# First attention: forget-gate bias as a row of the padded keys, output projection by rows, and the last value unit placed between the heads

## The chip, the cores and the metric

The kernel runs on one core of a Trainium2 chip. The core has a matrix engine (TensorE, PE in the profile), a vector engine (VectorE, DVE), an activation engine (ScalarE, ACT), GpSimd (POOL) and SyncE (SP), which issues most transfers. The engines run their own queues in order and wait for each other by semaphores. The metric is the device time of one execution in microseconds (us); lower is better.

## The reference

Two transformer blocks over 256 positions of width 1024, in float32. The change lies in the first layer of the first block:

```python
u = rms_norm(h, norm_mix[i]); m = rms_norm(mem, norm_mem[i])
q, k, v, f_logit, mq = split(u @ fox_w_in)          # 12 heads of 64, and 4 memory heads
q = rms_norm(q, fox_g_q); k = rms_norm(k, fox_g_k)
log_f = log_sigmoid(f_logit + fox_b_f)
c = cumsum(log_f, axis=1)
s = einsum('bqhd,bkhd->bhqk', q, k) * scale + (c[t] - c[s])   # causal
p = softmax(where(k_pos <= q_pos, s, NEG_INF)); o = p @ v
mem_out = memory_attention(mq, mk, mv, g_mq, g_mk)  # 256 memory tokens
h = h + concatenate([o, mem_out], -1) @ fox_w_out
z = rms_norm(h, norm_ffn[i]); h = h + swiglu(z, ...)
```

Behind it come a convolution layer with a mixture of experts, and a second block with differential and stick-breaking attention.

## The kernel before

**Exact products.** Each float32 weight unit (128 x 2048 numbers, 1 MB) is loaded into one of six buffers `raw`. ScalarE copies it to the reduced format (`wh`, the "hi" part, L736), then VectorE forms the rest (`wl`, "lo", L1671). This pair of instructions is called a split; there are three split buffers. `split_after(name)` splits the unit three places behind `name`, once `name` has been multiplied. A product is three matmuls (L1156 to L1158): hi x hi, hi x lo, lo x hi. Activations are split in the same way into `xh` and `xl`. A unit is 48 matmuls of 256 columns. `by_channels` and `by_tokens` multiply a unit whose columns are 256 outputs, over all 1024 inputs; `down` multiplies a unit of 256 input rows into all 1024 outputs, in four PSUM banks at once.

**Order around the change.** Units run in the order mk0, mv0, mq0 (memory), fq0 to fq2, fk0 to fk2, fv0 to fv2 (query, key, value of the 12 forget-gate heads, four heads to a unit), then 16 heads of attention (12 forget-gate, 4 memory), then fo0 to fo3 (output projection), norm sum number 2, and the feed-forward network (g0, u0, g1 and so on). During the projections, VectorE takes a reciprocal per query or key unit and scales it out of PSUM (`qk_scale`); keys go to `kz`, where each head has its 64 rows and 64 rows of zeros, so that one matmul over 128 rows can use a pair of heads' queries `qT` and see one head.

**The attention** is a loop over iterations i, written out on each engine (`attention` in the TensorE, ScalarE, VectorE code). `T_LAG` is 3 and `PV_LAG` is 4. In iteration i TensorE computes the scores of head i (L1287), for forget-gate heads with a second product that adds the bias -c[s] (L1290: `selh`, a one-hot of the head, times `negc`, the row of -c); transposes the probabilities of head i-3 (L1170); and multiplies those of head i-4 by the values (L1308, L1313). VectorE takes the scores out of PSUM into `att_p` with c[t] and the mask, but first waits for the transposes of head i-3, whose buffer it overwrites; then it takes the maxima (L1828) and the reciprocal of the row sums of head i-1. ScalarE takes the exponentials (L859) and copies the transposed head i-3 out of PSUM (L868). GpSimd scales the probabilities (L630, L632). When a pair of heads is complete, ScalarE copies it to `xh` (L873) and VectorE writes the low part `xl`.

`Sessions` assigns the PSUM banks by hand: each user of a bank waits (`claim`) until the one before has been drained. Scores alternate between banks 0 and 1, the transposes between 2 and 3, the pairs' outputs between 4 and 5. The splits that fall into the attention are placed by iteration, on both engines:

```python
FOX_SPLITS = {16: ("fv0",), 20: ("fv1", "fv2")}
attention(fox_maps, lambda i: [split_after(name) for name in FOX_SPLITS.get(i, ())])
```

So fo0 is split in iteration 16, fo1 and fo2 in 20; fo3, g0 and u0 are split while TensorE multiplies fo0 to fo3.

Of the kernel before, what the change touches and what calls it, by code (L numbers as in the profile page):

```python
# [202 lines left out]
def build(nc, x_dram, mem_dram, c_dram, cst_dram, cols_dram, main_dram, moe_dram, out):  # L203
    ctx = ExitStack()
    with ctx:
# [102 lines left out]
        selh = sqz[:, 0:FOX_HEADS * P].rearrange("p (h m) -> p h m", h=FOX_HEADS)  # L308
        negc = sqz[:, FOX_HEADS * P:FOX_HEADS * P + T]
# [41 lines left out]
        for j in range(1, 6):  # L351
            product(f"{'fq' if j < 3 else 'fk'}{j % 3}", j % 4)
            S.add(f"qsum{1 + j}", 4 + (1 + j) % 2)
        product("fv0", 7)
        S.add("qsum7", 5)
        product("fv1", 6)
        product("fv2", 2)
# [4 lines left out]
        def add_maps(kinds):  # L362
# [5 lines left out]
            dict(kind="fox" if h < FOX_HEADS else "mem", head=h, q=qT[:, h // 2, :], k=kz[:, h, :],  # L368
# [15 lines left out]
        FOX_SPLITS = {16: ("fv0",), 20: ("fv1", "fv2")}  # L384
# [4 lines left out]
        def add_attention(rng):  # L389
            n, a0 = len(rng), rng[0]  # L390
            for i in range(n + PV_LAG):
                if i < n:
                    S.add(f"sc{a0 + i}", (a0 + i) % 2)
                if 0 <= i - T_LAG < n:
                    S.add(f"pT{a0 + i - T_LAG}", 2 + (a0 + i) % 2)
                if 0 <= i - PV_LAG < n and (i - PV_LAG) % 2 == 0:
                    g = (a0 + i - PV_LAG) // 2
                    S.add(f"pv{g}", 4 + g % 2, own_signal=True)

        add_attention(fox_maps)  # L400
        for j in range(4):
            product(f"fo{j}", j)
        S.add("nsum2", 6)
# [204 lines left out]
        def _(pool):  # L608
# [11 lines left out]
            zero_keys(kz, "keys_zeroed")  # L620
            subtract_hi("x")
# [99 lines left out]
        def _(act):  # L721
# [110 lines left out]
            for j in range(6):  # L832
# [4 lines left out]
                if j == 0:  # L837

                    act.wait_ge(sem("negc_zeroed"), 1)
# [3 lines left out]
            for j in range(3):  # L843
                values_out(f"fv{j}", vv[:, :, T * j:T * j + T])
                if j == 0:
                    qk_sd(7)
            warm(ACT.Exp)

            def attention(rng, meanwhile=None, before=None):
                n, a0 = len(rng), rng[0]  # L850
                for i in range(n + PV_LAG + 1):
# [18 lines left out]
                    if 0 <= i - PV_LAG - 1 < n and (i - PV_LAG - 1) % 2 == 1 and maps[a0]["kind"] != "diff":  # L870
                        g = (a0 + i - PV_LAG - 1) // 2
# [6 lines left out]
            attention(fox_maps, lambda i: [split_after(name) for name in FOX_SPLITS.get(i, ())])  # L878

            warm(ACT.Sqrt)  # L880
            for j in range(4):
                wait_drained(act, f"fo{j}")
                square(hT, sqz, j)
                if j < 3:
                    split_after(f"fo{j}")
# [263 lines left out]
        def _(pe):  # L1149
# [125 lines left out]
            by_tokens("fv2")  # L1275

            def attention(rng, meanwhile=None):
                n, a0 = len(rng), rng[0]
                for i in range(n + PV_LAG):
                    if i < n:  # L1280
                        a = a0 + i
                        m, s = maps[a], bank(f"sc{a}")
                        full = m["kind"] == "mem"
                        claim(pe, f"sc{a}")
# [1057 lines left out]
```

## Time and profile before

| | us |
|---|---|
| median of 3 runs | 1910.46 (1907.53, 1910.46, 1910.5) |
| the profiled execution | 1907.86 |
| its span (first to last instruction) | 1906.0 |
| TensorE busy | 1802.0 (95%) |
| VectorE, ScalarE, GpSimd busy | 1443.3, 1171.6, 205.9 |
| first score of the first attention | 112.44 |
| output projection starts | 164.06 |
| root of norm sum 2 (ScalarE) | 190.83 |

In the profile's rows, L12 is line 12 of the kernel, `out<-in` are the tensors, `xN` the number of instructions merged into the row, and square brackets hold the idle time of the engine ahead of the row and the engine whose work ended it. A duration reaches to the end of the work; the next instruction of the engine can start somewhat before it. A float32 matmul counts as two instructions.

### The profile page before, as it was taken

The page shows a single profiled execution, that of the slowest core. Times are in us where ns is not written, and L with a number is a line of the kernel's source. Part 1 is how long each engine was busy: PE and PEld are TensorE (multiplying, and loading weights), DVE is VectorE, ACT ScalarE, POOL GpSimd, SP SyncE. Part 2 cuts the span into 40 slices and gives each one's busy share as a digit, 9 for nine tenths or more (in the row PEclk, how much of TensorE's full clock was granted, in tenths as well). Part 3 has the DMA queues.
Part 4 walks back from the last instruction along what each step waited for, and adds up shares of the span by engine and source line. Part 5 has one row for each costly group of instructions (what it writes and reads, how often), then busy time and mean ns, then how long its engine had stood idle before and what let it go on. Part 6 is the DMA issues. An engine that isn't in the chain of part 4 may idle for free.

```text
span 1906.0 us, 27557 instructions
## 1 busy us (share of the span) xinstructions
PE 1802.0 (95%) x10598; PEld 1583.3 (83%) x10598; DVE 1443.3 (76%) x1321; ACT 1171.6 (61%) x1141; POOL 205.9 (11%) x161
## 2 busy tenths in 40 slices
PE   6988899999899999999999999999999989689997
PEld 6977899999778878888788787887877889589997
DVE  6765687778758888888888888888889854765554
ACT  5435343455667777877777777777777744743332
POOL 2032111121120000000000000000006000403221
PEclk8999989999999999999999999999999999999999
DMA  7303798852139999999999999999999934035540
GB/s 310 136 23 145 295 400 323 317 199 89 67 142 388 373 357 390 367 385 378 360 390 364 384 376 361 391 366 382 377 358 417 370 130 155 1 121 189 177 155 23
DMA packets 74571, 520.84 MB, mean 273 GB/s; under 512 B 8064, under 2 KB 8192, under 8 KB 13952
## 3 DMA queue, kind: packets, MB, share of 16 engines
q1 hardware_dynamic: 73056, 514.02, 70.8%
q0 software_dynamic: 1440, 5.77, 0.8%
q8 instruction: 54, 0.88, 0.2%
q14 instruction: 21, 0.17, 0.0%
HBM read 504.02 MB, written 15.73 MB: 273 GB/s over the span
## 4 chain that ended last, share of the span: by engine, by line
PE 83%; DVE 7%; ACT 5%; DMA 2%; issue 2%; POOL 1%; ACTq 0%; DVEq 0%; SPq 0%
PE ps L1156 25%; PE ps L1158 24%; PE ps L1157 24%; DVE wl L1671 2%; PE ps L1358 1%; PE ps L1179 1%; DMA raw<-in_units 1%; ACT wh L1030 1%; PE ps L1526 1%; DMA raw<-in_experts 1%; DVE big L1664 1%; PE ps L1287 1%; DVE sqz L1664 1%; PE ps L1308 1%; ACT L1041 0%
## 5 line engine op out<-in xcount | busy, mean ns | idle before, releaser
L1671 DVE TENSOR_TENSOR wl<-raw,wh 128x2048 fp32r<-128x2048 f32 x446 | 1025.3, 2302 | 303.8 <-ACT wh L736 178.4
L1030 ACT ACTIVATE wh<-raw 128x2048 fp32r<-128x2048 f32 x336 | 643.2, 1918 | 180.5 <-PE ps L1158 176.5
L1156 PE MATMUL ps<-wh,xh 128*128 128x512 f32 (+1 forms) x1040 | 398.0, 383 | 9.6 <-DVE wl L1671 9.6
L1158 PE MATMUL ps<-wh,xl 128*128 128x512 f32 (+1 forms) x1040 | 390.2, 375 | 0.0
L1157 PE MATMUL ps<-wl,xh 128*128 128x512 f32 (+1 forms) x1040 | 389.7, 375 | 0.0
L1156 PE MATMUL ps<-xh,wh 128*128 128x256 f32 x1184 | 343.7, 290 | 25.0 <-DVE xl L1671 11.4
L1157 PE MATMUL ps<-xl,wh 128*128 128x256 f32 x1184 | 338.9, 286 | 0.0
L1158 PE MATMUL ps<-xh,wl 128*128 128x256 f32 x1184 | 338.7, 286 | 0.0
L736 ACT ACTIVATE wh<-raw 128x2048 fp32r<-128x2048 f32 x107 | 204.2, 1910 | 185.5 <-PE ps L1158 163.7
L1156 PEld LDWEIGHTS ps<-xh,wh 128*128 128x128 f32 x1184 | 231.4, 195 | 30.2 <-issue 23.7
L1156 PEld LDWEIGHTS ps<-wh,xh 128*128 128x128 f32 x1040 | 195.8, 188 | 50.9 <-DVE wl L1671 17.0
L1157 PEld LDWEIGHTS ps<-xl,wh 128*128 128x128 f32 x1184 | 231.6, 196 | 1.8 <-issue 1.7
L1158 PEld LDWEIGHTS ps<-xh,wl 128*128 128x128 f32 x1184 | 231.3, 195 | 0.0
L1158 PEld LDWEIGHTS ps<-wh,xl 128*128 128x128 f32 x1040 | 195.8, 188 | 35.9
L1157 PEld LDWEIGHTS ps<-wl,xh 128*128 128x128 f32 x1040 | 196.0, 188 | 34.0 <-issue 1.0
L1156 PE MATMUL ps<-wh,ah 128*128 128x512 f32 x448 | 175.9, 393 | 0.0
L1158 PE MATMUL ps<-wh,al 128*128 128x512 f32 x448 | 174.7, 390 | 0.0
L1157 PE MATMUL ps<-wl,ah 128*128 128x512 f32 x448 | 174.4, 389 | 0.0
L1156 PE MATMUL ps<-ah,wh 128*128 128x256 f32 x432 | 123.8, 287 | 6.5 <-DVE wl L1671 6.2
L1157 PE MATMUL ps<-al,wh 128*128 128x256 f32 x432 | 123.5, 286 | 0.0
L1158 PE MATMUL ps<-ah,wl 128*128 128x256 f32 x432 | 123.4, 286 | 0.0
L646 POOL TENSOR_TENSOR al<-att_p,ah 128x512 fp32r<-128x512 f32 x27 | 74.9, 2773 | 359.3 <-ACT ah L897 359.3
(292 smaller groups left out, 1933.9 us busy)
## 6 DMA issues: line engine op xcount, KB each, us to landing
raw<-in_experts SPq DMA_DIRECT2D x336, 1024.0 KB, 6.9
raw<-in_units SPq DMA_DIRECT2D x134, 1024.0 KB, 5.7
x_rows<-big SPq DMA_DIRECT2D x1, 6144.0 KB, 22.6
big<-x_rows SPq DMA_DIRECT2D x8, 512.0 KB, 7.9
y_rows<-big SPq DMA_DIRECT2D x7, 512.0 KB, 8.2
y_rows<-big SPq DMA_DIRECT2D x1, 2560.0 KB, 27.4
big<-in_mem SPq DMA_DIRECT2D x1, 1024.0 KB, 7.1
hT<-in_x SPq DMA_DIRECT2D x1, 1024.0 KB, 9.1
```

Of the source, the lines that this page charges most:

```text
L646: pool.tensor_tensor(al[:, c % 2, :], sg[:, c % 2, :], ah[:, c % 2, :].bitcast(F32), ALU.subtract).then_inc(sem("hid_lo"), 1)
L736: act.activation(wh[:, p % SPL, :], raw[:, n % RAW, :], ACT.Copy).then_inc(sem("hi_ready"), 1)
L1030: act.activation(wh[:, p % SPL, :], raw[:, n % RAW, :], ACT.Copy).then_inc(sem("hi_ready"), 1)
L1156: mm(out_, lh, rh, start=start, stop=False, **kw)
L1157: mm(out_, lh, rl, start=False, stop=False, **kw)
L1158: return mm(out_, ll, rh, start=False, stop=stop, **kw)
L1179: ins = mm(bank(f"nsum{k}")[:, 0:T], ones, src[:, T * j:T * j + T], start=(j == 0), stop=(j == KT - 1))
L1287: ins = mm(s[:, at:at + nk], m["q"][:, P * t:P * t + P], m["k"][:, 0:nk], start=True, stop=not fox)
L1308: mm(o[:, 0:T], m["v"][0], pT[:, 0:T], start=not second, stop=False, skip_group_check=True)
L1358: mm(bank(f"conv{c}")[:, 0:T], diag[:, n % DIAG_RING, :], upad[:, c, tap:tap + T], start=(tap == 0), stop=(n + 1 == taps_through(PE_CONV, ...
L1664: return V.scalar_tensor_tensor(out=out_, in0=in0, scalar=scalar, in1=in1, op0=op0, op1=op1)
L1671: return V.tensor_tensor(out_, whole, leading.bitcast(F32), ALU.subtract)
```

## The change

1. The bias becomes a row of the padded keys. GpSimd sets the zero rows of the queries to zero and one of them to one (`qT` for even heads; a new `q_odd`, laid over `normed`, for odd heads), and two DMAs bring -c into that row of `kz`. The second product of each score goes, as do `selh` and the copy that made it. `negc` moves into `plan_f`. The queries are scaled in two halves of 64 partitions.
2. The output projection's weights are laid out by rows (`units_by_rows`): half a unit holds the weights of one pair of heads, for all outputs. `fo_rows(g)` multiplies pair g in iteration 2g + 6, between the transposes and the value product, and the last pair behind the loop, into banks 4 to 7.
3. The last value unit fv2 is multiplied in iterations 0 and 2 (`last_values`), its values copied out in 3.
4. To make room, the transposes all use bank 2 and the pairs' outputs bank 3. A pair's output is copied out one iteration earlier (`out_lag` is `PV_LAG`). The waits for queries, keys and values are spread over the heads.
5. The splits move to iterations 2 (fo0), 5 (fo1), 7 (fo2), 10 (fo3), 14 (g0) and 18 (u0).

```diff
@@ sessions and splits
-        FOX_SPLITS = {16: ("fv0",), 20: ("fv1", "fv2")}
+        FOX_SPLITS = {2: ("fv0",), 5: ("fv1",), 7: ("fv2",), 10: ("fo0",), 14: ("fo1",), 18: ("fo2",)}
-                    S.add(f"pT{a0 + i - T_LAG}", 2 + (a0 + i) % 2)
+                    S.add(f"pT{a0 + i - T_LAG}", turned[(a0 + i) % len(turned)])
-                    S.add(f"pv{g}", 4 + g % 2, own_signal=True)
-        add_attention(fox_maps)
+                    S.add(f"pv{g}", out[g % len(out)], own_signal=True)
+        add_attention(fox_maps, (2,), (3,))
         for j in range(4):
-            product(f"fo{j}", j)
-        S.add("nsum2", 6)
+            product(f"fo{j}", 4 + j)
+        S.add("nsum2", 3)
@@ GpSimd
+            wait_lo(pool, "mem0")
+            pool.wait_ge(sem("keys_zeroed"), 1)
+            pool.memset(qT[HD:P, 0:FOX // P, :], 0.0).then_inc(sem("queries_zeroed"), 1)
+            pool.wait_ge(sem("queries_zeroed"), 1)
+            pool.memset(qT[HD:HD + 1, 0:FOX // P, :], 1.0).then_inc(sem("queries_one"), 1)
             subtract_hi("x")
...
-            pool.memset(negc, 0.0).then_inc(sem("negc_zeroed"), 1)
+            pool.memset(q_odd[0:HD, :, :], 0.0).then_inc(sem("queries_zeroed"), 1)
+            pool.memset(q_odd[0:1, :, :], 1.0).then_inc(sem("queries_one"), 1)
+            pool.wait_ge(sem("negc_ready"), 1)
+            for odd in range(2):
+                pool.dma_start(kz[HD * (1 - odd):HD * (1 - odd) + 1, odd:FOX_HEADS:2, :],
+                               negc[odd:FOX_HEADS:2, :]).then_inc(sem("bias_rows"), 16)
@@ TensorE
-                            if fox:
-                                ins = mm(s[:, at:at + nk], selh[:, m["head"], :], negc[:, 0:nk],
-                                         start=False, stop=True)
+            def beside_fox(i):
+                if i in (0, 2):
+                    last_values(i // 2)
+                if i % 2 == 0 and i >= 6:
+                    fo_rows((i - 6) // 2)
+            attention(fox_maps, turned=beside_fox, ready=fox_ready, values=values_ready)
+            fo_rows(KT - 1)
             norm_sum(2)
@@ VectorE
-                    V.tensor_copy(selh, ident[:, 0:FOX_HEADS].unsqueeze(2).broadcast_to([P, FOX_HEADS, P])).then_inc(
-                    qk_scale(f"fq{j - 1}", [(qT[:, 2 * j - 2:2 * j, :], 0, P, gq8[:, 0:1])])
+                    qk_scale(f"fq{j - 1}", [(qT[0:HD, 2 * j - 2:2 * j, :], 0, HD, gq8[:, 0:1]),
+                                            (q_odd[HD:P, 2 * j - 2:2 * j, :], HD, P, gq8[:, 0:1])])
```

How the instructions stand now. TensorE before, one iteration in the middle of the attention (scores with bias, transposes, value product); `drained2` and `drained3` are the banks of the transposes:

```order
L1287 MATMUL ps<-big 128x128 [waits drained0]
L1290 MATMUL ps<-sqz 128x128
L1287 MATMUL ps<-big 128x256
L1290 MATMUL ps<-sqz 128x256
L1170 MATMUL ps<-cst,att_p 128x128 [waits drained2,att_probs]
L1170 MATMUL ps<-cst,att_p 128x128 x2
L1308 MATMUL ps<-att_pT,big 64x256 [waits drained3,drained4]
L1313 MATMUL ps<-att_pT,big 64x128
```

TensorE after, iteration 6 and the start of 7; lines 1172 to 1174 are the matmuls of half a unit of fo, 24 in all, of which the first three are shown:

```order
L1321 MATMUL ps<-big 128x128 [waits drained0]
L1321 MATMUL ps<-big 128x256
L1186 MATMUL ps<-cst,att_p 128x128 [waits drained2,att_probs]
L1186 MATMUL ps<-cst,att_p 128x128 x2
L1172 MATMUL ps<-xh,wh 128x256 [waits drained7,lo_ready,drained6,drained3,drained5,drained4]
L1173 MATMUL ps<-xl,wh 128x256
L1174 MATMUL ps<-xh,wl 128x256
...
L1343 MATMUL ps<-att_pT,big 64x256 [waits drained2,drained3]
L1348 MATMUL ps<-att_pT,big 64x128
L1321 MATMUL ps<-big,sqz 128x128 [waits drained1]
...
L1186 MATMUL ps<-cst,att_p 128x128 [waits drained2,att_probs]
```

The bias products are gone, half a unit of fo stands between transposes and value product, and each set of transposes waits for `drained2`, the drain of the one before. VectorE before, iteration 5 and the start of 6: the scores of the next head follow the reciprocal of the sums at once:

```order
L1664 SCALAR_TENSOR_TENSOR att_p<-ps,ctok,cst 128x128 [waits filled3,filled1]
L1813 TENSOR_SCALAR att_p<-ps,ctok 128x128
L1664 SCALAR_TENSOR_TENSOR att_p<-ps,ctok,cst 128x128
L1828 TENSOR_REDUCE nmx<-att_p 128x1 [waits drained1]
L1828 TENSOR_REDUCE nmx<-att_p 128x1
L1833 RECIPROCAL rsum<-ssum 128x2 [waits att_exp]
L1664 SCALAR_TENSOR_TENSOR att_p<-ps,ctok,cst 128x128 [waits filled2,filled0]
```

VectorE after, iteration 5 and the start of 6:

```order
L1727 SCALAR_TENSOR_TENSOR att_p<-ps,ctok,cst 128x128 [waits filled2,filled1]
L1875 TENSOR_SCALAR att_p<-ps,ctok 128x128
L1727 SCALAR_TENSOR_TENSOR att_p<-ps,ctok,cst 128x128
L1890 TENSOR_REDUCE nmx<-att_p 128x1 [waits drained1]
L1890 TENSOR_REDUCE nmx<-att_p 128x1
L1895 RECIPROCAL rsum<-ssum 128x2 [waits att_exp]
L1734 TENSOR_TENSOR xl<-ps,xh 128x256 [waits mix_hi]
L1734 TENSOR_TENSOR wl<-raw,wh 128x2048 [waits hi_ready]
L1727 SCALAR_TENSOR_TENSOR att_p<-ps,ctok,cst 128x128 [waits filled2,filled0]
```

The low part of a weight split now stands between two heads' softmax instructions, behind a wait for ScalarE's high part (`hi_ready`), in iterations 2, 5, 7, 10, 14 and 18.

## Rows read from the trace of the kernel before

**Rows 1.** The page, part 1: TensorE busy us, share, instructions.

```profile
PE 1802.0 (95%) x10598; PEld 1583.3 (83%) x10598; DVE 1443.3 (76%) x1321; ACT 1171.6 (61%) x1141; POOL 205.9 (11%) x161
```

**Rows 2.** Windows, projections and attention: busy us (instructions) by engine, clock, DMA.

```profile
60.00:112.40 52.40, 51.35 (x397) 48.25 (x397) 45.14 (x25) 20.14 (x24) 0.00 (x0) 1.00 0.36 127
112.40:163.00 50.60, 41.63 (x228) 30.09 (x228) 29.27 (x96) 27.66 (x91) 25.34 (x32) 1.00 0.00 1
```

**Rows 3.** Chain of waits of TensorE, 90 to 190 us: us, times, longest.

```profile
PE ps L1308 <- ACT att_pT L868: 8.0, 7, 2.1
```

**Rows 4.** Timeline, TensorE, one head: start us, duration us, instruction.

```profile
122.48 0.62 PE L1308 MATMUL ps<-att_pT,big 128*64 128x256 f32 x2 [1.52 <-ACT att_pT L868]
...
123.24 0.49 PE L1287 MATMUL ps<-big 128*128 128x128 f32 x2
123.57 0.39 PE L1290 MATMUL ps<-sqz 128*128 128x128 f32 x2
123.79 0.60 PE L1287 MATMUL ps<-big 128*128 128x256 f32 x2
124.22 0.59 PE L1290 MATMUL ps<-sqz 128*128 128x256 f32 x2
124.66 0.49 PE L1170 MATMUL ps<-cst,att_p 128*128 128x128 f32 x3
```

**Rows 5.** Timeline of the same head: VectorE, ScalarE (copies apart), TensorE.

```profile
125.25 0.35 DVE L1664 SCALAR_TENSOR_TENSOR att_p<-ps,ctok,cst 128x128 f32<-128x128 f32 x1 [2.60 <-PE ps L1170]
...
126.80 0.40 ACT L859 ACTIVATE att_p<-att_p,nmx 128x128 f32<-128x128 f32 x1 [2.83 <-DVE nmx L1828]
...
127.70 0.47 ACT L868 ACTIVATE att_pT<-ps 128x384 f32<-128x384 f32 x1
...
128.31 0.62 PE L1308 MATMUL ps<-att_pT,big 128*64 128x256 f32 x2 [0.53 <-ACT att_pT L868]
```

**Rows 6.** Timeline, a weight split inside the attention: ScalarE, then VectorE.

```profile
158.33 1.91 ACT L736 ACTIVATE wh<-raw 128x2048 fp32r<-128x2048 f32 x1
...
160.27 2.29 DVE L1671 TENSOR_TENSOR wl<-raw,wh 128x2048 fp32r<-128x2048 f32 x1 [1.37 <-ACT wh L736]
```

**Rows 7.** Timeline, from the last value product to the second norm.

```profile
162.86 0.38 ACT L873 ACTIVATE xh<-ps 128x256 fp32r<-128x256 f32 x1 [0.89 <-PE ps L1310]
...
164.06 0.36 PE L1156 MATMUL ps<-xh,wh 128*128 128x256 f32 x1 [1.24 <-DVE xl L1671]
...
190.83 0.47 ACT L758 ACTIVATE rn<-ps,cst 128x256 f32<-128x256 f32 x1 [2.10 <-PE ps L1179]
```

**Rows 8.** Timeline, VectorE in the projections: query scaling, key scaling, last keys.

```profile
81.64 2.29 DVE L1671 TENSOR_TENSOR wl<-raw,wh 128x2048 fp32r<-128x2048 f32 x1 [0.27 <-ACT wh L736]
...
87.23 0.75 DVE L1664 SCALAR_TENSOR_TENSOR big<-ps,gq,att_p 128x512 f32<-128x512 f32 x1
...
93.83 1.51 DVE L1664 SCALAR_TENSOR_TENSOR big<-ps,cols,att_p 64x512 f32<-64x512 f32 x2
...
105.90 1.51 DVE L1664 SCALAR_TENSOR_TENSOR big<-ps,cols,att_p 64x512 f32<-64x512 f32 x2
```

**Rows 9.** Timeline, GpSimd: zeroing of the keys, and the low parts of x.

```profile
0.71 3.51 POOL L611 MEMSET big<- 128x4096 f32 x1 [0.29 <-POOLq L2332]
37.14 10.04 POOL L617 TENSOR_TENSOR xl<-sqz,xh 128x256 fp32r<-128x256 f32 x5 [32.92 <-ACT xh L773]
```

**Rows 10.** Timeline, TensorE after a pause of 4.09 us, and 3 us later.

```profile
194.88 0.55 PE L1156 MATMUL ps<-xh,wh 128*128 128x256 f32 x1 [4.09 <-DVE xl L1671]
...
195.44 0.41 PE L1158 MATMUL ps<-xh,wl 128*128 128x256 f32 x1
195.66 0.41 PE L1156 MATMUL ps<-xh,wh 128*128 128x256 f32 x1
...
198.22 0.28 PE L1157 MATMUL ps<-xl,wh 128*128 128x256 f32 x1
198.34 0.28 PE L1158 MATMUL ps<-xh,wl 128*128 128x256 f32 x1
```

More of the change, by code:

```diff
@@ L350, in build @@
         S.add("cum", 6)
-        for j in range(1, 6):
-            product(f"{'fq' if j < 3 else 'fk'}{j % 3}", j % 4)
+        for j, b in zip(range(1, 6), (0, 1, 2, 3, 6)):
+            product(f"{'fq' if j < 3 else 'fk'}{j % 3}", b)
             S.add(f"qsum{1 + j}", 4 + (1 + j) % 2)
@@ L355, in build @@
         S.add("qsum7", 5)
-        product("fv1", 6)
-        product("fv2", 2)
+        product("fv1", 4)
+        product("fv2", 7)
         maps = []
@@ L367, in build @@
         fox_maps = add_maps([
-            dict(kind="fox" if h < FOX_HEADS else "mem", head=h, q=qT[:, h // 2, :], k=kz[:, h, :],
+            dict(kind="fox" if h < FOX_HEADS else "mem", head=h,
+                 q=(q_odd if h % 2 and h < FOX_HEADS else qT)[:, h // 2, :], k=kz[:, h, :],
                  v=[vv[:, t, HD * h:HD * h + HD] for t in range(TT)], row=HD * (h % 2), m=HD, to=h // 2)
@@ L387, in build, with add_attention @@
         DIFF_SPLITS = {9: "sv0", 10: "sv1"}
-        def add_attention(rng):
+        def add_attention(rng, turned=(2, 3), out=(4, 5)):
             n, a0 = len(rng), rng[0]
@@ L842, in _, with attention @@
                                    scale=-1.0).then_inc(sem("negc_ready"), 1)
[L843 to L846, printed above, removed]
+            values_out("fv0", vv[:, :, 0:T])
+            qk_sd(7)
+            values_out("fv1", vv[:, :, T:2 * T])
             warm(ACT.Exp)
-            def attention(rng, meanwhile=None, before=None):
+            def attention(rng, meanwhile=None, before=None, out_lag=PV_LAG + 1):
                 n, a0 = len(rng), rng[0]
@@ L876, in attention @@
                         meanwhile(i)
-            attention(fox_maps, lambda i: [split_after(name) for name in FOX_SPLITS.get(i, ())])
+            def beside_fox(i):
+                if i == 3:
+                    values_out("fv2", vv[:, :, 2 * T:3 * T])
+                for name in FOX_SPLITS.get(i, ()):
+                    split_after(name)
+            attention(fox_maps, beside_fox, out_lag=PV_LAG)
             warm(ACT.Sqrt)
@@ L1274, in _, with fox_ready, values_ready, attention @@
             by_tokens("fv1")
-            by_tokens("fv2")
-            def attention(rng, meanwhile=None):
+            def fox_ready(h):
+                if h == FOX_HEADS:
+                    wait_drained(pe, "mk0")
+                    wait_drained(pe, "mq0")
+                elif h < FOX_HEADS and h % 4 == 0:
+                    wait_drained(pe, f"fq{h // 4}")
+                    wait_drained(pe, f"fk{h // 4}")
+            def values_ready(h):
+                if h == FOX_HEADS:
+                    wait_drained(pe, "mv0")
+                elif h < FOX_HEADS and h % 4 == 0:
+                    wait_drained(pe, f"fv{h // 4}")
+                if h == 0:
+                    wait_drained(pe, "fk1")
+            def attention(rng, turned=None, ready=None, values=None, meanwhile=None):
                 n, a0 = len(rng), rng[0]
@@ L1850, in _ @@
             dve.wait_ge(sem("ld_cst_rest"), 16)
-            attention(fox_maps, lambda i: [split_after(name) for name in FOX_SPLITS.get(i, ())])
+            attention(fox_maps, lambda i: [split_after(name) for name in FOX_SPLITS.get(i, ())], PV_LAG)
             def residual(name, j):
```

78 lines of the change are left out of this document (50 added, 28 removed).

## The prediction

> **What bounds the kernel now.** I read the page first: TensorE is busy 95% of the span [rows 1], so a change pays only by taking work off TensorE or by filling its pauses. Windows over the stretch that the diff touches then show two regimes [rows 2]. In the projections TensorE is busy 51.35 of 52.40 us, and VectorE 45.14: TensorE bounds, with VectorE close behind. In the attention TensorE is busy 41.63 of 50.60 us and no engine is full: a chain bounds it. The chain of waits names it: TensorE's value product waits for ScalarE's copy of the transposed probabilities, 7 times, 8.0 us in all [rows 3]. The timeline of one head [rows 5] gives its links, counted from the start of the three transposes at 124.66 [rows 4]: VectorE may take the next head's scores at 125.25 (0.59 later, because it overwrites the buffer that the transposes read), ScalarE's exponentials start 1.55 later at 126.80, its copy 0.90 later at 127.70, and the copy ends 0.47 later, at 128.17; TensorE moves at 128.31. That is 3.65 us from one transpose to the moment when its PSUM copy is out. The two banks of the transposes (2 and 3) let the next head's transposes start before that, so that two heads take about 5.9 us (122.48 to 128.31 [rows 4, 5]).
>
> **What the change removes.** The bias products: 0.22 us (123.57 to 123.79) and 0.44 us (124.22 to 124.66) per head [rows 4], 0.66 x 12 = 7.9 us of TensorE. What can be won by filling pauses too is 50.60 - 41.63 = 9.0 us of attention and the 1.24 us ahead of the output projection [rows 2, 7].
>
> **What it moves on TensorE.** fv2 and the output projection keep their matmuls, 48 to a unit, one each 0.12 us (198.22 to 198.34 [rows 10]): 5.76 us a unit, 2.88 us a half. fv2's halves lie in iterations 0 and 2, the halves of fo in iterations 6, 8 to 18 and one behind. By rows instead of by columns costs nothing: as many products of the same shape.
>
> **What it adds on GpSimd.** Four fills of 1536 columns; a fill of 4096 took 3.51 us [rows 9], so 1.3 us each. The first two lie ahead of x's low parts, but GpSimd is idle for 32.92 us up to 37.14 [rows 9]. The last two and the two small DMAs start at about 48 and 63 us, and the first score now stands at about 105.5: even 10 us each hides. Without that cover a late row would hold the first score, and TensorE with it, by the same time. Bounds: 0 to 1 us; I take 0.
>
> **VectorE in the projections.** Each of three query units is scaled in two halves of 64 partitions, 1.51 us for the two, instead of one of 0.75 [rows 8]: +0.76 x 3 = 2.3 us. Its waits there (0.27 us a unit [rows 8], about 0.7 in three) absorb a part; the mask copy that goes lies ahead of a longer wait. So VectorE leaves the last keys at 105.90 + 1.51 + 1.6 = 109.0 instead of 107.4. Before, 5 us of fv2 covered that; now head 0's softmax waits for it.
>
> **The new chain.** The transposes now share bank 2. The transposes of one head can start only when the copy of the head before is out, and VectorE takes new scores only behind them. The 3.65 us thus become the least distance between neighbouring transposes: call it the short step. If a half of fo stands in between (every second step from iteration 6), TensorE's own work is longer: transposes 0.4, 0.3 waiting for the low part of the head pair, 2.88, value product 0.76, scores 0.76 (0.33 + 0.43 [rows 4]), in sum 5.1 to 5.2: the long step. A pair costs 3.6 + 5.2 = 8.8. Before it cost 5.9, and the fo half 2.88 behind: 8.8 as well. The removed 0.66 us per head therefore turns into waiting, but for the ends.
>
> At this place a rule stands against the change. The Trainium skill, Perfetto Trace Analysis, section Matmuls, says that independent groups of matmuls should rotate through PSUM banks, so that the evacuation of one overlaps the next. The trace agrees as to what the second bank does (two heads in 5.9 us rather than 2 x 3.65 = 7.3). By the rule alone, the lost overlap would be 7.3 - 5.9 = 1.4 us a pair, about 10 us in seven pairs, less the 7.9 us of bias products: +2 us. The sum below, which also charges the splits, does not use this figure.
>
> **Splits.** Before, one weight split ran in iteration 16 and two in 20, behind the last softmax, and the rest beside fo, where ScalarE and VectorE had time. Now they run in iterations 2, 5, 7, 10, 14 and 18. A split is 1.91 us on ScalarE (158.33) and then 2.29 us on VectorE (160.27), one after the other [rows 6]. Both engines run in order, so VectorE takes the next head only behind both. From the transposes of an iteration with a split, VectorE is free after 0.59 + 1.55 + 0.90 + 0.37 (+0.28 where a pair's output is copied, in odd iterations) + 1.90 + 2.24 = 7.55 (7.83), and the transposes two steps later come 3.06 us behind that (1.55 + 0.90 + 0.47 + 0.14): 10.6 (10.9) for two steps instead of 8.8. Cost 1.8 or 2.0 us each for iterations 5, 7, 10 and 14, because the fo half covers only a part. The one in iteration 2 stands in the filling of the pipe, where nothing covers it. The one in iteration 18 is behind the last softmax and costs nothing.
>
> **The sum**, on the clock of the trace of before. VectorE: heads 0, 1, 2 from 109.0, 1.43 each, maximum of head 2 at 113.4; exponentials to 114.3; ScalarE's split to 116.2; VectorE's to 118.5; head 3: 1.55, 0.90 and head 0's copy 0.47, so head 1's transposes stand at 121.6 (iteration 4), while TensorE has waited since 115.6. Transposes of iteration 5: 125.2; 7: 136.1; 9: 147.0; 10: 150.6; 12: 161.2; 13: 166.4; 14: 170.0; 16: 180.6. Then there is no softmax left: 17 at 185.0 (0.4 + 0.3 + 2.88 + 0.8), 18 at 186.2. Tail: 3.6 for transposes and fo half, 1.5 for two value products, 1.24 for the hand-over [rows 7], 2.88 for the last half, 3.7 for the norm sum (190.83 - 164.06 less four units of 5.76 [rows 7]): 199.2. The same reckoning over the order of before, started at its first score, ends 0.8 us ahead of the row at 190.83, so I add 0.8. For the clock I add 0.6: behind a pause of 4.09 us the matmuls came each 0.22 us (195.44 to 195.66), and 0.12 us three microseconds later [rows 10]; there are now one pause of 5.9 us and two between 3 and 4, and most of the slow work falls into further waiting. Sum 200.6 against 190.83: **+9.8 us**. All that follows is unchanged and TensorE-bound, and shifts with it. The sum stands against the profiled execution, 1907.86 us (span 1906.0): 1917.7. The median of the runs lies 2.6 us above that execution; I take half of it and say 1919.
>
> **Rivals.**
> A. The splits hide and only the one bank costs. Without the five costs (3.6 in the filling, 2.0, 2.0, 1.8, 1.8 = 11.2) the end is at 189.4, or -1.4 us: about 1908 to 1909, within 0.2% of before. For it: ScalarE is busy only 27.66 us and VectorE 29.27 of 50.60 [rows 2]. Against: at 158.33 and 160.27 they ran one after the other, VectorE having waited 1.37 us for ScalarE's half [rows 6]. It decides if VectorE has two heads' scores in hand ahead of a split, which needs transposes more than 4 us ahead.
> B. Faster: TensorE stays full from 105.5. Its work is then 41.6 - 7.9 (attention less bias), + 5.76 + 23.04 + 3.7 = 66.2 us, end at 171.7; with 3 us for the first softmax and 1.2 for the hand-over 176, or -15 us: 1894. It decides if the chain per pair is shorter than TensorE's work per pair (6.6 us). For it: TensorE has something to do in every second iteration. Against: the two links of 3.65 us in a row, 7.3 us.
> C. The long pauses cost more, because the slow clock also falls on the fo halves (2.88 becomes 5.1), three times 2.2 us, and VectorE's splits also delay the pair's low part: +6 us over the forecast, 1925.
>
> **Chances.** Forecast (1914 to 1923) 0.69; A 0.14; B 0.07; C 0.10. A run of this kernel differs by 3.0 us among three (1907.53 to 1910.5), so 0.2% or 3.8 us is about what can be told from no change. Slower by more than 0.2% (above 1914.3): 0.79, the forecast and C; within: 0.14, A; faster: 0.07, B. The range 1911 to 1927 takes in the forecast, C and the upper end of A.
>
> **What would show it.** In the profile after: no bias row beside the scores; a first score at about 105.5 and a TensorE pause of 5 to 6 us before head 1's transposes; transposes' starts apart by 3.6 and 5.2 us in turn, and 10.6 to 10.9 for two where a split lies between; waits of the transposes for the copy of the transposed probabilities, in sum near 25 us, instead of the value product's 8.0; the second norm's root at 200 to 201 instead of 190.83; nothing changed behind that. I am wrong if VectorE has no scores waiting while it runs its splits (A), or if TensorE's busy time fills the window (B).

## The result and the profile after

| | before | after |
|---|---|---|
| median, us | 1910.48 (4 runs, 1907.53 to 1912.92) | 1923.66 (4 runs, 1923.03 to 1926.43) |
| profiled execution, us | 1907.86 | 1926.43 |
| its span | 1906.0 | 1924.3 |
| root of norm sum 1, root of norm sum 2 | 30.67, 190.83 | 31.59, 205.46 |
| from one root to the other ("the stretch") | 160.16 | 173.87 |

After / before is 1.007, interval 1.0058 to 1.0082: slower by 13.2 us. 13.7 us of that lie in the stretch between the two roots, which holds the memory head start, all projections, the attention and the output projection. The rest of the 18.3 us by which the two profiled spans differ (0.9 ahead of the stretch, 3.7 behind) I put down to these two executions: the one of before lies 2.6 us under its median, the one of after 2.8 over.

The page after, part 1, and the chain of waits of TensorE from 90 to 206 us (us, times, longest):

```profile
PE 1805.9 (94%) x10550; PEld 1582.9 (82%) x10550; DVE 1445.8 (75%) x1323; ACT 1172.6 (61%) x1141; POOL 213.4 (11%) x166
```

```profile
PE ps L1186 <- ACT att_pT L880: 22.5, 9, 6.2
PE ps L1172 <- DVE xl L1734: 2.6, 7, 1.1
```

The second line is TensorE's wait for the low part of a pair's output. TensorE has 48 instructions less [rows 1] and yet is busy 3.9 us longer: the work that is left took longer. Where the value product waited 8.0 us in all [rows 3], the transposes (L1186) now wait 22.5 us for the copy of the transposed probabilities, which empties their one bank.

Timeline of TensorE after: starts of the transposes, from iteration 4 on (start, duration, in brackets the idle time ahead and what ended it):

```profile
122.67 0.87 PE L1186 MATMUL ps<-cst,att_p 128*128 128x128 f32 x3 [6.18 <-ACT att_pT L880]
126.70 0.88 PE L1186 MATMUL ps<-cst,att_p 128*128 128x128 f32 x3
...
137.95 0.52 PE L1186 MATMUL ps<-cst,att_p 128*128 128x128 f32 x3 [1.74 <-ACT att_pT L880]
141.62 0.52 PE L1186 MATMUL ps<-cst,att_p 128*128 128x128 f32 x3 [1.51 <-ACT att_pT L880]
...
148.84 0.52 PE L1186 MATMUL ps<-cst,att_p 128*128 128x128 f32 x3 [1.73 <-ACT att_pT L880]
152.51 0.52 PE L1186 MATMUL ps<-cst,att_p 128*128 128x128 f32 x3 [1.51 <-ACT att_pT L880]
...
163.14 0.52 PE L1186 MATMUL ps<-cst,att_p 128*128 128x128 f32 x3 [2.97 <-ACT att_pT L880]
...
170.12 0.49 PE L1186 MATMUL ps<-cst,att_p 128*128 128x128 f32 x3
...
173.84 0.52 PE L1186 MATMUL ps<-cst,att_p 128*128 128x128 f32 x3 [1.37 <-ACT att_pT L880]
...
184.70 0.63 PE L1186 MATMUL ps<-cst,att_p 128*128 128x128 f32 x4 [3.93 <-ACT att_pT L880]
```

The short step is there: 137.95 to 141.62 and 148.84 to 152.51 are 3.67 us each. Two steps with a split in them: 137.95 to 148.84 is 10.89 us, 152.51 to 163.14 is 10.63. The split itself, in iteration 2 (ScalarE, VectorE, VectorE's next softmax):

```profile
115.49 1.89 ACT L750 ACTIVATE wh<-raw 128x2048 fp32r<-128x2048 f32 x1
117.41 2.29 DVE L1734 TENSOR_TENSOR wl<-raw,wh 128x2048 fp32r<-128x2048 f32 x1 [2.78 <-ACT wh L750]
119.62 0.35 DVE L1727 SCALAR_TENSOR_TENSOR att_p<-ps,ctok,cst 128x128 f32<-128x128 f32 x1
```

VectorE stands 2.78 us for ScalarE's half, then does its own, and head 3 is taken from PSUM only at 119.62. In [rows 6] the same pair ran behind the last softmax, where nobody waited for it. One thing is new. Windows of after (the seventh value is the granted clock):

```profile
120.00:125.00 5.00, 2.33 (x8) 1.31 (x8) 2.49 (x10) 1.84 (x6) 1.50 (x2) 0.56 0.63 210
125.00:130.00 5.00, 4.11 (x16) 2.36 (x15) 1.78 (x8) 2.13 (x8) 2.14 (x4) 0.76 0.00 0
...
165.00:170.00 5.00, 5.00 (x25) 4.37 (x24) 0.31 (x2) 1.47 (x5) 1.50 (x2) 0.66 0.01 3
...
185.00:190.00 5.00, 4.90 (x28) 4.55 (x26) 0.35 (x2) 0.60 (x1) 1.82 (x2) 0.66 0.15 59
```

The granted clock is 1.00 in all windows of before from 105 to 190 us; after, it falls in three places, each at one of the long pauses (6.18, 2.97 and 3.93 us). In windows of 1 us it falls between 120 and 121 us, inside the first pause, and at 165 and between 185 and 186, when TensorE had been at work again for 2 and for 1 us. Its price is seen where half a unit of fo begins and the value product follows, once behind such a pause and once not (after, TensorE):

```profile
163.87 0.36 PE L1172 MATMUL ps<-xh,wh 128*128 128x256 f32 x1 [0.21 <-DVE xl L1734]
...
168.36 0.65 PE L1343 MATMUL ps<-att_pT,big 128*64 128x256 f32 x2
...
174.57 0.36 PE L1172 MATMUL ps<-xh,wh 128*128 128x256 f32 x1 [0.21 <-DVE xl L1734]
...
177.61 0.65 PE L1343 MATMUL ps<-att_pT,big 128*64 128x256 f32 x2
```

The half of fo between 163.87 and 168.36 took 4.5 us, the one between 174.57 and 177.61 3.0; the one behind the third pause (185.43 to 189.96) 4.5 again.

### The profile page after: what moved, and what is told of

It is laid out like the page before. It is cut to its first block, busy times and chain, and to the rows that moved or that the text cites. A ratio compares the mean times of both kernels' runs of the same rounds, so it can differ in the third digit from the quotient of the medians.

```text
span 1924.3 us, 27470 instructions
## 1 busy us (share of the span) xinstructions
PE 1805.9 (94%) x10550; PEld 1582.9 (82%) x10550; DVE 1445.8 (75%) x1323; ACT 1172.6 (61%) x1141; POOL 213.4 (11%) x166
## 4 chain that ended last, share of the span: by engine, by line
PE 79%; DVE 9%; ACT 6%; issue 3%; DMA 2%; POOL 1%; ACTq 0%; DVEq 0%; SPq 0%; POOLq 0%
PE ps L1172 24%; PE ps L1174 23%; PE ps L1173 23%; DVE wl L1734 3%; PE ps L1421 2%; PE ps L1195 1%; DMA raw<-in_units 1%; ACT wh L1046 1%; PE ps L1589 1%; DVE att_p L1801 1%; ACT wh L750 1%; DVE big L1727 1%; DMA raw<-in_experts 1%; DVE sqz L1727 1%; ACT att_p L871 1%
```

## The experiments

All were run beside the kernel before, whose median was between 1910.4 and 1911.4 us in each group. "Stretch" is root to root in the profiled execution, 160.16 before and 173.87 after.

| kernel | median us (runs) | ratio to before | stretch |
|---|---|---|---|
| after | 1923.66 (4) | 1.007 (1.0058 to 1.0082) | 173.87 |
| e1 after, small splits | 1913.24 (1) | | 163.78 |
| e2 after, VectorE's half later | 1917.4 (10) | 1.0028 (1.0017 to 1.004) | 164.78 |
| e3 before, one transpose bank | 1923.71 (4) | 1.0065 (1.0048 to 1.0082) | 172.33 |
| e4 before, bias row | 1911.38 (11) | 1.0003 (0.9994 to 1.0012) | 160.13 |
| e5 after, pauses filled | 1925.05 (4) | 1.007 (1.0053 to 1.0086) | 173.07 |
| e6 bias row, fv2 between, fo behind | 1905.48 (7) | 0.9969 (0.9958 to 0.998) | 154.52 |
| e7 e4, pauses filled | 1907.95 (11) | 0.9988 (0.9979 to 0.9997) | 156.81 |
| e8 e6, pauses filled | 1905.97 (10) | 0.9976 (0.9967 to 0.9985) | 155.14 |
| e9 e6, copy first | 1896.99 (5) | 0.9934 (0.9921 to 0.9948) | 147.58 |
| e10 e2, copy first | 1905.3 (6) | 0.9975 (0.9962 to 0.9987) | 157.76 |

The theory, as predicted: the splits inside the softmax chain cost about 11 us, the single transpose bank sets a step of 3.65 us, and the saved bias products turn into waiting. Rival A: the splits are hidden. A second rival came with the result: a lower clock behind pauses.

**e1: are the splits the loss?** After, with the six splits in the first attention cut to 8 of 2048 columns, so that the other columns of those six units are stale: the work of the splits is left out.

```diff
-                    split_after(name)
...
+                    act.activation(wh[:, p % SPL, 0:8], raw[:, n % RAW, 0:8], ACT.Copy).then_inc(sem("hi_ready"), 1)
...
+                    rest(wl[:, p % SPL, 0:8], raw[:, n % RAW, 0:8], wh[:, p % SPL, 0:8]).then_inc(sem("lo_ready"), 1)
```

> The changed kernel, but each of the six weight splits inside the first attention copies and subtracts only 8 of 2048 columns on ScalarE and VectorE (all waits and signals stay), so fo, g0 and u0 are multiplied with stale weights: what is left out is the splitting of these units. Because later values change, only the trace up to the root of norm sum 2 is to be read (205.46 us in the changed kernel, of which 0.9 is its later start). Theory (splits stand in the softmax chain, plus the slow clock after the pauses that they make): 191 to 192.5, that is 13 to 14.5 us earlier, with no TensorE pause above 2 us inside the attention. Rival (the halves of the output projection between transposes and value products are the cost, and splits hide beside them): at most 3 us earlier.

Measured: a stretch of 163.78 us, 10.1 less than after, against 13 to 14.5 for the theory and at most 3 for rival A (one execution). TensorE's waits for the copy fell from 22.5 to 11.6 us:

```profile
PE ps L1189 <- ACT att_pT L880: 11.6, 7, 2.5
```

The splits do not hide, and A is refuted. Which share of the loss is theirs can't be said: 10.1 us go with them here, and 12.2 come with the single bank alone in e3, so the two overlap. The clock was low here too: below 1.00 in seven of the 5-us windows between 115 and 180 (0.54 in that from 120 to 125), although the longest wait for the copy was 2.5 us. That is what the expectation missed.

**e2: is it the work of the split, or where it stands?** After, with VectorE's half one iteration later than ScalarE's. Nothing is left out.

```diff
-            attention(fox_maps, lambda i: [split_after(name) for name in FOX_SPLITS.get(i, ())], PV_LAG)
+            attention(fox_maps, lambda i: [split_after(name) for name in FOX_SPLITS.get(i - 1, ())], PV_LAG)
```

> The changed kernel, with VectorE's half of each of the six splits one iteration later (behind the softmax of the next head), ScalarE's half where it was. Theory (VectorE stands still for ScalarE's copy before each subtraction, and the next head behind it): the wait of 2.8 us per split goes, the pauses on TensorE with it; about 12 us faster than the changed kernel, 1911 to 1913, so about the time of before. Rival (the 2.3 us of VectorE's work itself is what delays, wherever it stands, or the interleaved projection is): within 3 us of the changed kernel, 1921 to 1924.

Measured: a stretch of 164.78 us, 9.1 less than after, though every split is done in full. VectorE's half of the first one no longer waits (e2, VectorE):

```profile
116.90 2.27 DVE L1734 TENSOR_TENSOR wl<-raw,wh 128x2048 fp32r<-128x2048 f32 x1
```

In after, VectorE stood for ScalarE's half ahead of all six splits (2.78, 1.38, 1.38, 3.16, 3.27 and 2.17 us); in e2 it stands ahead of none. So it was the wait of one engine in front of the other's half, and not the 4.2 us of work. The median, 1917.4, missed the expected 1911 to 1913: its runs spread from 1910.71 to 1919.92, at a mean clock of 0.983 in the fastest and 0.978 in the slowest. In the profiled one the clock is below 1.00 in eight of the twelve 5-us windows between 120 and 180, though TensorE is busy for most of some of them (first value 5.00 is the window, then TensorE's busy time):

```profile
120.00:125.00 5.00, 3.98 (x13) 2.24 (x12) 2.22 (x9) 1.70 (x7) 2.25 (x4) 0.50 0.63 210
125.00:130.00 5.00, 4.90 (x31) 3.84 (x31) 3.30 (x8) 4.45 (x12) 2.52 (x3) 0.82 0.01 3
...
135.00:140.00 5.00, 4.65 (x27) 4.47 (x27) 4.17 (x8) 3.42 (x7) 2.83 (x3) 0.70 0.01 3
```

**e3: the single transpose bank by itself.** Before, with all transposes of the first attention in bank 2.

```diff
-                    S.add(f"pT{a0 + i - T_LAG}", 2 + (a0 + i) % 2)
+                    S.add(f"pT{a0 + i - T_LAG}", turned[(a0 + i) % len(turned)])
-        add_attention(fox_maps)
+        add_attention(fox_maps, (2,))
```

> The kernel before with a single edit: the transposes of the first attention all use bank 2. Theory (one bank makes every step between transposes the full 3.65 us chain, where before two heads took 5.9): 1.4 us a pair plus the delay of iteration 16's split, 9 to 10 us slower than before, 1919 to 1921. Rival (the chain of before runs through VectorE and ScalarE anyway, so the bank is free in time): within 2 us of before.

Measured: 1923.71 us, a stretch 12.2 us longer than before; this edit alone costs as much as the whole change. TensorE's starts of the transposes (e3) and its waits:

```profile
131.73 0.52 PE L1170 MATMUL ps<-cst,att_p 128*128 128x128 f32 x3 [0.86 <-ACT att_pT L868]
135.41 0.52 PE L1170 MATMUL ps<-cst,att_p 128*128 128x128 f32 x3 [0.86 <-ACT att_pT L868]
139.08 0.52 PE L1170 MATMUL ps<-cst,att_p 128*128 128x128 f32 x3 [0.86 <-ACT att_pT L868]
```

```profile
PE ps L1170 <- ACT att_pT L868: 14.9, 12, 2.5
```

These heads take 3.68 us each, the later ones up to 3.75: the short step, forecast as 3.65. The lower clock (0.72 from 125 to 130 us, 0.88 and 0.78 from 165 to 175) accounts for the 2 us above the expected 9 to 10: the step from 123.80 to 128.08 took 4.28 us instead of 3.68, and that from the transposes at 168.96 to those at 171.88, with no wait in it, 2.92 instead of 1.59 (before, 158.81 to 160.40). The rule of the Trainium skill, Perfetto Trace Analysis, section Matmuls, to rotate independent groups through PSUM banks, is borne out for this order of ScalarE's work. A pair takes 7.36 us against 5.83 of before, 1.5 more where I had estimated 1.4; what goes beyond the 9 to 10 us expected for the whole stretch is the lower clock. e10 shows what the price depends on.

**e4: the bias row by itself.** Before, with part 1 of the change alone (the fills, the two DMAs, the split scaling of the queries; the bias products go).

```diff
-                            ins = mm(s[:, at:at + nk], m["q"][:, P * t:P * t + P], m["k"][:, 0:nk],
-                                     start=True, stop=not fox)
-                            if fox:
-                                ins = mm(s[:, at:at + nk], selh[:, m["head"], :], negc[:, 0:nk],
-                                         start=False, stop=True)
+                            ins = mm(s[:, at:at + nk], m["q"][:, P * t:P * t + P], m["k"][:, 0:nk],
+                                     start=True, stop=True)
```

> The kernel before with the bias as a row of the padded keys and nothing else of the change (fills, two small DMAs, halved query scaling, no second product; two transpose banks, fv2 and the projection where they were, splits in iterations 16 and 20). Theory (before, TensorE's 5.2 us for two heads lie in a chain of about 5.9, and 0.43 to 0.66 us of bias product per pair stands on it): 3 us faster than before, 1907 to 1909. Rival (all of the freed matmul time turns into waits for the copy, as in the changed kernel, and VectorE's 2.3 us of extra scaling shows): no change or 1 us slower, 1910 to 1912.

Measured: no change (1.0003), as the rival had it and not the theory. Yet the heads did come faster: three pairs take 16.2 us (132.65 to 148.85), 5.4 each, where before had three in 17.5 (134.49 to 151.99), 5.8 each. TensorE's value products (e4):

```profile
132.65 0.62 PE L1317 MATMUL ps<-att_pT,big 128*64 128x256 f32 x2 [1.59 <-ACT att_pT L881]
...
148.85 0.62 PE L1317 MATMUL ps<-att_pT,big 128*64 128x256 f32 x2 [1.10 <-ACT att_pT L881]
...
154.69 0.62 PE L1317 MATMUL ps<-att_pT,big 128*64 128x256 f32 x2 [2.12 <-ACT att_pT L881]
156.96 1.11 PE L1317 MATMUL ps<-att_pT,big 128*64 128x256 f32 x2
```

The last row took 1.11 us for what takes 0.65: the clock was 0.66 in the windows from 120 to 125 and from 155 to 160. Before had a pause of the same 2.12 us and kept its clock (before, TensorE; then the 5 us up to the end of that pause in before, and in e4):

```profile
157.83 0.62 PE L1308 MATMUL ps<-att_pT,big 128*64 128x256 f32 x2 [2.12 <-ACT att_pT L868]
```

```profile
152.83:157.83 5.00, 2.88 (x17) 2.02 (x17) 2.01 (x6) 3.13 (x12) 3.22 (x4) 1.00 0.01 3
149.69:154.69 5.00, 2.88 (x17) 2.02 (x17) 2.01 (x6) 3.13 (x12) 3.22 (x4) 1.00 0.01 3
```

TensorE's busy time (the second value) is the same in these 5 us, and it is the same in the 5 us ahead of them (3.90 us in both kernels) and in the 5 before those (3.68). So neither the pause nor the work in the 15 us up to its end tells why the clock fell in one and not in the other.

**e5: pauses of after filled.** After, with products of the zero rows of the keys (32 partitions) ahead of the transposes: five in iteration 12, seven in iteration 16, into a bank where they add zero.

```diff
+            def zero_products(i):
+                for _ in range({12: 5, 16: 7}.get(i, 0)):
+                    mm(bank("fo0")[:, 0:T], cst[96:P, C_ONES:C_ONES + P], kz[96:P, 0, :], start=False, stop=False,
+                       skip_group_check=True)
```

> The changed kernel with matmuls of zeros in the two long TensorE pauses of iterations 12 and 16 (5 and 7 of 256 columns over 32 rows, adding zero to the bank of fo0; the output stays as it was). Theory (the 3.0 and 3.9 us pauses are followed by a granted clock at its lower level, which makes two fo halves 1.5 us longer each): 3 us faster, 1920 to 1921. Rival (the time behind the pauses is set by the chain, not by TensorE's clock): no change or up to 1 us slower, 1923 to 1925.

Measured: 0.8 us off the stretch instead of 3, and nothing in the median, as the rival had it. Behind the first fill the fo half took 3.0 us (163.54 to 166.57), as at full clock. The clock fell during the second fill (1.00 to 181 us, 0.85 from 181 to 182, 0.50 behind), and the fo half behind it took 5.2 us (183.64 to 188.84) instead of 4.5 (e5):

```profile
178.89 3.63 PE L1396 MATMUL ps<-big,cst 32*128 32x256 f32 x14
182.90 1.09 PE L1186 MATMUL ps<-cst,att_p 128*128 128x128 f32 x4 [0.38 <-ACT att_pT L880]
```

So it settles at most half of the question: behind one fill the clock stayed, and the step was 1.5 us shorter; behind the other it did not, and the step was 0.7 us longer.

**e7: the same question on e4, with full products.** e4, with two products over all 128 rows into the unused bank 7 ahead of every second value product of iterations 4 to 16; their result is not used.

```diff
+                        if a0 == 0 and a % 2 == 0 and 4 <= i <= 16:
+                            for _ in range(2):
+                                mm(ps[:, 7, 0:T], ident, kz[:, 0, :], start=True, stop=True)
```

> The kernel before with the bias row alone (as in the run of that edit, which gave no change), and two extra products of 256 columns over all 128 rows (their result in an unused bank is read by nobody) ahead of every second value product from iteration 4 to 16, where TensorE waits 1.1 to 2.1 us. Theory (the bias row wins 2 to 3 us in the chain, and a lower granted clock, at 120 to 125 and 155 to 160 us of that run, takes them back because TensorE now pauses more): with the pauses filled the clock stays at its full level, and the kernel is 2 us faster than before, 1908 to 1909.5. Rival (the chain alone sets the time; the clock's level is incidental): 1911 to 1912, as without the fill, or slower if the fill delays a value product.

Measured: 1907.95 us, as expected, 2.5 less than before in its group; a stretch 3.35 us shorter than before's. TensorE does more work than in e4 and is done earlier. Windows of e4 (first two) and of e7 (last two):

```profile
120.00:125.00 5.00, 4.67 (x17) 3.04 (x18) 1.91 (x8) 1.59 (x7) 1.95 (x3) 0.66 0.00 0
155.00:160.00 5.00, 5.00 (x19) 2.50 (x18) 2.72 (x2) 3.13 (x5) 1.72 (x2) 0.66 0.00 0
```

```profile
120.00:125.00 5.00, 4.28 (x25) 2.98 (x24) 2.63 (x11) 2.61 (x10) 2.88 (x5) 1.00 0.02 3
155.00:160.00 5.00, 3.76 (x20) 2.05 (x19) 3.05 (x3) 3.80 (x6) 1.80 (x3) 1.00 0.19 26
```

The clock stays at 1.00 from 105 to 190 us. This is not one execution alone: the mean clock over the whole program was 0.983 or 0.984 in all eleven runs of e7 and 0.981 or 0.982 in all eleven of e4. Of the 3.3 us between the two stretches, 1.7 lie in the step from the last pause on (e4 154.69 to 162.64, e7 153.54 to 159.80) and 1.0 in the pair with the first low window (120.33 to 126.47 against 121.00 to 126.11). Another 0.66 lie in the next pair, where both clocks are 1.00 (6.18 against 5.52 us), and what makes them is not shown. So the lower clock takes most of what the bias row gains back in e4; what the fill does to the kernel before, without the bias row, was not run.

**e6: what of the change pays.** After, with fo by columns behind the attention again, its two banks each, and its splits in iterations 16 and 20 as before; it keeps the bias row, fv2 in iterations 0 and 2, and the earlier output copy.

```diff
-        FOX_SPLITS = {2: ("fv0",), 5: ("fv1",), 7: ("fv2",), 10: ("fo0",), 14: ("fo1",), 18: ("fo2",)}
+        FOX_SPLITS = {16: ("fv0",), 20: ("fv1", "fv2")}
-        add_attention(fox_maps, (2,), (3,))
+        add_attention(fox_maps)
-                if i % 2 == 0 and i >= 6:
-                    fo_rows((i - 6) // 2)
-            fo_rows(KT - 1)
+            for j in range(4):
+                by_channels(f"fo{j}")
```

> The changed kernel with the output projection taken out of the attention again: by columns, behind the last head, banks 0 to 3, so that the transposes have banks 2 and 3 and the outputs 4 and 5, with the splits in iterations 16 and 20 and beside the projection as before. What stays of the change is the bias row and fv2 in iterations 0 and 2 (and the outputs copied out one iteration earlier). Theory (bank and splits were the whole loss; fv2 fills the wait for the first softmax): 6 to 7 us faster than before, 1903.5 to 1905.5, and some 19 us faster than the changed kernel. Rival (fv2's halves between the first heads delay them by what they save, or VectorE's later end of the key scaling at 109 instead of 107.4 is not covered): no better than the bias row alone, 1907 to 1911.

Measured: 1905.48 us and a stretch of 154.52, 5.64 less than before and 19.35 less than after. The bias row, which gave nothing alone (e4), and fv2 in the pause of the first softmax pay together; moving fo, with what it needs (one bank each, splits between the heads), turns these -5.6 us into +13.7.

**e8: pauses of e6 filled.** e6 with the fill of e7 into bank 6, iterations 8 to 16.

```diff
+                        if a0 == 0 and a % 2 == 0 and 8 <= i <= 16:
+                            for _ in range(2):
+                                mm(ps[:, 6, 0:T], ident, kz[:, 0, :], start=True, stop=True)
```

> The kernel with bias row and fv2 between the heads but the projection behind (6 us faster than before), with the same two extra products ahead of every second value product in iterations 8 to 16. Theory: the stretch at the lower clock behind iteration 15 (0.66 of full speed from 150 to 155 us) goes, 1 to 1.5 us faster than without, 1904 to 1905. Rival: 1905.5 or slower.

Measured: 1905.97 us, nothing gained on e6, as the rival had it. The window from 150 to 155 us, at 0.66 in e6, is now at 1.00, but the one from 120 to 125, ahead of the fills, came at 0.69 where e6 had 1.00. It neither supports nor refutes the theory of the clock, but it shows something else. Up to there e6 and e8 are the same program, with the same pause (e6, then e8):

```profile
118.97 0.62 PE L1345 MATMUL ps<-att_pT,big 128*64 128x256 f32 x2 [2.16 <-ACT att_pT L880]
```

```profile
118.20 0.62 PE L1348 MATMUL ps<-att_pT,big 128*64 128x256 f32 x2 [2.15 <-ACT att_pT L880]
```

Behind it e6 stayed at 1.00 and e8 fell to 0.50, from 120 to 123 us. So the same instructions and pauses can end either way, and a single trace doesn't tell what an edit does to the clock.

**e9: the link of the chain that can go.** In both kernels ScalarE takes the exponentials of head i ahead of the copy of head i-3. In [rows 5] it is idle for 2.83 us ahead of the exponentials at 126.80, while the transposes that it has to copy, begun at 124.66 [rows 4], were done before VectorE took the next scores at 125.25. e9 is e6 with the two blocks exchanged, in all three attentions.

```diff
+                    if 0 <= i - T_LAG < n:
+                        a = a0 + i - T_LAG
...
                     if i < n:
                         a = a0 + i
                         w0, w1 = (P, 3 * P) if maps[a]["kind"] != "mem" else (T, 2 * T)
                         act.wait_ge(sem("att_max"), 2 * (a + 1))
...
-                    if 0 <= i - T_LAG < n:
-                        a = a0 + i - T_LAG
...
```

> The kernel with bias row and fv2 between the heads but the projection behind, with one more edit: in each iteration ScalarE copies the transposed probabilities out of PSUM ahead of the exponentials of the next head instead of behind them (in all three attentions that use this loop). Theory (the chain runs through ScalarE's fixed order: the copy is ready 2.4 us before ScalarE comes to it): the wait of the value products goes, about 5.5 us less in the first attention, 1899 to 1901 in all, more if the other attentions gain too. Rival (VectorE's and GpSimd's part of the chain is next and as long): 1904 to 1906.

Measured: 1896.99 us, 13.4 less than before, better than expected, and the fastest of all. TensorE's waits (e9, 90 to 206 us):

```profile
PE ps L1174 <- DVE xl L1737: 5.5, 2, 4.1
PE ps L1188 <- POOL att_p L646: 3.7, 5, 1.4
PE ps L1323 <- DVE att_p L1730: 0.3, 1, 0.3
```

No wait for the copy is left; two pairs of heads take 9.46 us (transposes at 130.43, 135.29 and 139.89), the clock is 1.00 from 105 to 175 us, and the stretch is 147.58, 6.9 us shorter than e6's (which had a window at 0.66). The second block's first attention is shorter too: 1604.45 to 1628.90 us, 24.45 us against 27.14 in e6.

**e10: the same exchange with one bank, fo between the heads and the splits.** e2, with the exchange of e9 in all three attentions.

```diff
-            attention(fox_maps, lambda i: [split_after(name) for name in FOX_SPLITS.get(i, ())], PV_LAG)
+            attention(fox_maps, lambda i: [split_after(name) for name in FOX_SPLITS.get(i - 1, ())], PV_LAG)
@@ ScalarE's attention: the two blocks exchanged as in e9
```

> The changed kernel with VectorE's half of each split one iteration later (5 us slower than before) and ScalarE's copy ahead of the exponentials. Theory (with one transpose bank, what makes a short step 3.65 us is that the copy stands behind VectorE's softmax and the exponentials; without that it is about 1.1 us, and the single bank costs nothing): 5 to 9 us faster than without this edit, 1908 to 1912, and the steps between transposes no longer 3.65 us. Rival (one bank costs by itself): 1915 or more.

Measured: 1905.3 us, better than the expected 1908 to 1912 (12.1 us under e2's median, whose runs were at a low clock), and a stretch 7.0 us shorter than e2's. The transposes and the waits (e10):

```profile
138.56 0.49 PE L1186 MATMUL ps<-cst,att_p 128*128 128x128 f32 x3
140.53 0.49 PE L1186 MATMUL ps<-cst,att_p 128*128 128x128 f32 x3
147.15 0.49 PE L1186 MATMUL ps<-cst,att_p 128*128 128x128 f32 x3
```

```profile
PE ps L1172 <- DVE xl L1734: 15.1, 9, 4.1
PE ps L1186 <- ACT att_pT L872: 1.4, 1, 1.4
```

The short step falls from 3.65 to 1.97 us (1.1 was expected) with the same single bank, as short as the shortest of e9 with two (118.73 to 120.71): the bank was dear in that step because its copy stood behind the exponentials. The wait has moved to the low part of the pair's output (`xl`), for which each fo half now waits (15.1 us, 4.1 of it behind norm sum 2), and a pair takes 8.6 us against e9's 4.7 and its fo half of 2.88 behind. Even so arranged, fo between the heads is 8.3 us behind e9 (10.2 in the stretch).

## Why the prediction was right, and where it was off

The time was forecast as 1919.0, 8.5 us over the median of before, from +9.8 in the stretch; it was 1923.66, +13.2, and +13.7 in the stretch. That is within the stated 1911 to 1927, but 0.7 us above the forecast's own band (1914 to 1923), and nearer to rival C's 1925, which had a chance of 0.10. The mechanism was the forecast's; that the total still fell into the range owes something to its width. Step by step:

- **Starts.** First score forecast at 105.5: it was 106.47 in a trace whose norm root 1 came 0.92 later, so 105.5. VectorE's first softmax forecast at 109.0: 110.14, less 0.92 is 109.2. The fills and DMAs of GpSimd lay in its idle time, as forecast.
- **Short step.** 3.65 forecast, 3.67 in after, 3.68 in e3. Right.
- **Steps with a split.** 10.9 (iterations 7 to 9) and 10.6 (10 to 12) forecast, 10.89 and 10.63 in the rows; 5.9 us of pause ahead of iteration 4 forecast, 6.18 measured. All splits: 11.2 forecast, 10.1 by e1, and 9.1 by e2 for VectorE's waits alone (both with a lower clock of their own). Waits for the copy: 25 forecast, 22.5.
- **The clock: the term that was mis-sized.** "For the clock I add 0.6", because "most of the slow work falls into further waiting". Where a fo half follows a long pause nothing waits, and it is on the path. Against the forecast's steps the rows are late by 1.8 us from 163.14 to 170.12 (6.98 for 5.2) and by 1.9 from 184.70 to 190.97 (6.27 for 4.4), of which each fo half is 1.5; the two steps behind 122.67 add 0.4 and 0.35 (4.03 us each instead of 3.67). The clock thus cost about 3.7 us where I had allowed 0.6: 3.1 of the difference of 3.9. What is left of the two long steps (0.3 and 0.4, at full clock) and 0.7 on the rest of the path make 1.4 where the reckoning's correction was 0.8; the start was 0.15 late.
- **Its premise was wrong too, not only its size.** I took it that only pauses of 3 us or more matter. e1, e2 and e4 fell to a lower clock with no wait above 2.54 us in the attention, where before, with the same 2.12 us at 157.83, has no low window. A saving on TensorE inside a chain-bound stretch can so cost clock; e4 and e7 show it over eleven runs each.
- **Rivals.** A (splits hidden) fell by e1 and e2. B (TensorE full) fell by the trace: TensorE was busy 74.52 of the 100 us from 105 to 205. C had two mechanisms for its +6 us: the clock on fo halves is real, on two halves at 1.5 us instead of three at 2.2; a delay of the pair's low part is not seen (2.6 us of waits in seven, as much as the 0.3 each of the forecast).

**What is left open.** What exactly lets the clock fall: equal pauses with equal work ahead of them ended differently (before and e4, 2.12 us; e6 and e8, 2.16 and 2.15), and two fills of e5 as well; only e7 holds it, with full products in every second head. The fills without the bias row were not run. And why the runs of e2 spread over 9 us; mean clock and time roughly go together there (0.983 at 1910.71, 0.976 to 0.979 from 1915.3 up), which is a correlation. That the 8 us between e9 and e10 are the low part's wait alone was not tried: banks and splits differ as well.

## What to carry to other kernels

Where a chain bounds a stretch, look first at the order inside each in-order engine for a short instruction that others wait for behind a long one that is ready later: exchanging two blocks was worth 8.5 us here in the median (e9 on e6; in the profiled executions 6.9 in the stretch and 2.7 in the second block's first attention), more than any of the moved work gained. Work put between the heads pays if it brings no wait of one engine for another into the chain and takes no buffer from it (fv2), and costs more than it fills if it does (fo with its splits and single banks). A saving on TensorE that becomes pauses may come back as a lower clock, so check the granted clock before and after, over several executions.

## What was unexpected of the hardware

The granted clock went down to 0.54, 0.50 and 0.66 in 5-us windows behind waits of at most 2.5 us (e1, e2, e4), not only behind the 4.09 us of [rows 10]. Of two executions with the same instructions up to that point and the same pause of 2.2 us, it fell in one and not in the other (e8 and e6). In it a 256-column matmul comes every 0.21 us instead of 0.12 (1.2 GHz of the two levels, 1.2 and 2.4), and a fo half takes 4.5 to 5.2 us instead of 3.0. Two unused products ahead of every second value product made a kernel faster: 1907.95 us against 1911.38 (e7 and e4; 0.9988 and 1.0003 of before in their groups).
